# Samples' attention of a hybrid decoder layer: scores moved one step behind the key transposes, three PSUM banks for them, and the first gate block taken out of the Strassen loop

## The reference, cut to what matters

```python
def nsa_sample(nq, kvc, kvs, kvw, ngate, pool_c, pool_s, win_buf, page_table):
    ...
    o_c, imp = compressed_branch(qg, kc, q_pos)
    idx, valid = select_blocks(imp, q_pos, n_sel)
    ...
    o_s = sel_attend(qg, kv_sel, idx, valid, q_pos)
    o_w, win_new = window_sample(qg, win_buf, kvw, q_pos)
    return nsa_combine(o_c, o_s, o_w, ngate), win_new

def merge_out(o_hg, o_nsa, mgate, w_out):
    g = jax.nn.sigmoid(mgate.astype(jnp.float32)).reshape(B, T, N_BRANCH, D_MODEL)
    u = g[:, :, 0] * o_hg + g[:, :, 1] * o_nsa
    return u.astype(o_hg.dtype) @ w_out
```

## Time and profile before

| | |
|---|---|
| three runs, us | 1932.56, 1938.71, 1940.87 (median 1938.71) |
| the profiled execution: time / span of the trace, us | 1931.92 / 1930.1 |
| PE busy in the span | 1753.9 us (91%), 9667 matmuls |
| DVE, ACT, POOL busy | 49%, 27%, 33% |
| mean granted TensorE clock | 0.942 |
| samples' attention, first key transposes to first gate product | 855.1 to 1227.1 us |
| the eight gate blocks | 1227.1 to 1337.3 us |
| lines L2047, L2092, L2070 (PE busy) | 88.1, 83.3, 86.2 us |

### The profile page before, as it was taken

The page is one execution under the profiler, slowest core; times in us unless marked ns, Lnnn a source line. Parts: engine busy times, 40 slices in busy tenths (PEclk is TensorE's granted clock), DMA queues, the critical chain, the costliest instruction groups (busy, mean ns, idle before and its releaser), DMA issues.

```text
span 1930.1 us, 25763 instructions
## 1 busy us (share of the span) xinstructions
PE 1753.9 (91%) x9667; PEld 1229.7 (64%) x9667; DVE 953.7 (49%) x1702; ACT 522.8 (27%) x1114; POOL 634.5 (33%) x634
## 2 busy tenths in 40 slices
PE   7999999989979799976788887998989999999996
PEld 6777777777857555653555555776467777763332
DVE  6767776672000367753454445233267777760003
ACT  3122222221010245533444445211222222220101
POOL 2344443431000322235565552141045556530000
PEclk9999999998979579988999999999989999999998
DMA  8677666664430100014776677432043232311111
GB/s 262 217 241 241 230 204 227 229 207 163 109 118 4 45 1 1 2 45 148 220 227 208 211 227 235 128 110 87 28 109 88 66 88 66 88 66 54 66 41 49
DMA packets 201014, 248.81 MB, mean 129 GB/s; under 512 B 32201, under 2 KB 173850, under 8 KB 192538
## 3 DMA queue, kind: packets, MB, share of 16 engines
q1 hardware_dynamic: 176684, 134.16, 23.8%
q0 software_dynamic: 21248, 109.46, 16.5%
q10 hardware_dynamic: 2960, 3.54, 0.5%
HBM read 236.09 MB, written 19.29 MB: 132 GB/s over the span
## 4 chain that ended last, share of the span: by engine, by line
PE 74%; DVE 11%; DMA 5%; issue 4%; ACT 3%; another core or an unknown queue 2%; ACTq 1%; SPq 0%; POOL 0%; DVEq 0%; POOLq 0%
PE ps L2118 21%; PE ps L2244 8%; PE ps L1735 7%; DVE mem L1247 4%; PE ps L2070 4%; PE ps L1746 4%; DMA mem<-in_cache_cmp_kv,pidx 4%; PE ps L2092 3%; PE ps L2183 3%; PE ps L2047 3%; PE ps L1767 3%; PE ps L1975 2%; PE ps L1996 2%; PE ps L1962 2%
## 5 line engine op out<-in xcount | busy, mean ns | idle before, releaser
L2118 PE MATMUL ps<-mem 128*128 128x288 f32 x1352 | 338.2, 408 | 0.8 <-DVE mem L1185 0.8
L2118 PEld LDWEIGHTS ps<-mem 128*128 128x128 f32 x1352 | 256.2, 191 | 70.7 <-DVE mem L1185 1.0
L734 POOL DMA_INDIRECT mem<-in_cache_sel_kv,sidx x192 | 186.1, 969 | 322.0 <-PE ps L1928 174.3
L1735 PE MATMUL ps<-mem 128*128 128x288 f32 x1024 | 269.7, 426 | 14.7 <-DVE mem L1273 13.6
L1735 PEld LDWEIGHTS ps<-mem 128*128 128x128 f32 x1024 | 203.6, 200 | 73.7 <-issue 14.6
L1247 DVE TENSOR_TENSOR mem<-mem 128x2048 f32<-128x2048 f32 x56 | 159.6, 2850 | 43.3 <-DMA mem<-in_cache_cmp_kv,pidx 42.7
L697 POOL DMA_INDIRECT mem<-in_cache_cmp_kv,pidx x56 | 90.4, 1615 | 239.5 <-DVE mem L1247 210.6
L2244 PE MATMUL ps<-mem 128*128 128x512 f32 x352 | 163.7, 608 | 0.0
L2092 PE MATMUL ps<-mem 128*64 128x512 f32 x288 | 83.3, 654 | 61.0 <-ACT mem L1032 35.9
L1519 DVE TENSOR_TENSOR mem<-ps,mem 128x512 f32<-128x512 f32 x64 | 44.3, 692 | 153.4 <-PE ps L2092 92.2
L2244 PEld LDWEIGHTS ps<-mem 128*128 128x128 f32 x352 | 63.9, 191 | 80.7 <-issue 80.6
(11 more groups left out here) (363 smaller groups left out, 2687.2 us busy)
## 6 DMA issues: line engine op xcount, KB each, us to landing
mem<-in_cache_sel_kv SPq DMA_DIRECT2D x320, 128.0 KB
mem<-in_w_up SPq DMA_DIRECT2D x44, 512.0 KB, 5.1
mem<-in_w_in SPq DMA_DIRECT2D x32, 512.0 KB, 7.5
mem<-in_w_in SPq DMA_DIRECT2D x14, 1024.0 KB, 5.2
mem<-in_w_down SPq DMA_DIRECT2D x10, 1024.0 KB, 5.0
mem<-in_state_win_kv SPq DMA_DIRECT2D x16, 512.0 KB
out<-in_state_win_kv POOLq DMA_DIRECT2D x8, 1008.0 KB, 15.8
mem<-in_x_prompt SPq DMA_DIRECT2D x8, 512.0 KB, 5.4
```

What stands on the lines that cost most here:

```text
L734: pool.indirect_dma_start(kring[kq % NKR][:, j, :], None, pool_rows, bass.IndirectOffsetOnAxis(sidx[:, i:i + 1], 0)).then_inc(pg_g[kq % NK ...
L1735: mm = t.matmul(ps[:, 2 * (u % 2) + a, 0:NHF], lhs(k), hT[:, k, a * NHF:(a + 1) * NHF], start=(k == 0), stop=(k == KD - 1))
L2118: mm = t.matmul(ps[:, bank, 0:NHF], lhs[:, k, :], rhs[:, k, :], start=(first and k == 0), stop=(k == KD // 2 - 1), skip_group_check=True)
```

## The change

It renames and re-times, and computes the same.

- PE: the scores of step `s - 1` are issued in step `s`, after the values (`scores(n)`, called as the last piece before the compressed branch). The transposed keys go in two halves into three banks in turn (0, 1, 5; `KB`), each with its own semaphore step; probabilities have bank 4 alone.
- ACT: two copies of 512 columns instead of one of 1024, into three pairs of buffers; before the next transposes of probabilities PE waits for the copy of the last ones.
- `LAG` is 17 and `VAHEAD` 4. The exponentials move to `c` 1 to 4, DVE's scaling to 5 to 7. `e_c1`, `e_c3` move to `c` 1, 2; `e_c2` to 1, `e_c5` to 4, `e_c4`, `e_c6`, `e_c8`, `e_c10` to 2, 4, 6, 8. `e_out` stays tied to `LAG`.
- SP: the three blocks of gate weights come at `s` = 77, 79 and 81 instead of together at 80.
- The first gate block is done as 32 plain matmuls in two halves (`gate0`) in steps 84 and 86, with its sigmoids in ACT's steps 86 and 88; the loop of seven products has seven blocks left.

The diff, cut to its core (left out are re-numbered counts of `mp`, `mg_v`, `mg_a` in the gate loop, and the semaphores' names):

```diff
@@ -76,9 +76,9 @@
-LAG = NC + 6
+LAG = NC + 7
 K_POOL = (0, 1, 2)
-KAHEAD, VAHEAD = 4, 3
+KAHEAD, VAHEAD = 4, 4
...
@@ -217,7 +217,9 @@
-        kTs = [view(2 * PGC * P).rearrange("p (g n) -> p g n", g=2) for _ in range(2)]
+        kTs = [[view(PGC * P) for _ in range(2)] for _ in range(2)]
+        kTs.append([avm[:, :, :, :].rearrange("p i r c -> p (i r c)"), scanm[:, 0:PGC * P]])
+        KB = (0, 1, 5)
...
@@ -226,7 +228,7 @@
-        psm, psg, pscT = view(P), view(P), [view(P) for _ in range(2)]
+        psm, psg, pscT = view(P), view(P), [view(P) for _ in range(2)] + [hmask[:, :]]
...
@@ -478,7 +482,7 @@
-                return mp, 7 * (b - B_MG) + 7
+                return (mp, 7 * (b - B_MG)) if b > B_MG else (m0p, 2)
...
@@ -602,7 +606,7 @@
-                        wait(sp, ek_ok, kq - NKR + 1)
+                        wait(sp, ek_ok, 2 * (kq - NKR + 1))
...
@@ -610,10 +614,10 @@
-                if s == NC * SB:
-                    sp.wait_ge(ek_ok, SB * (NPC + 1))
-                    for b in range(B_MG, B_MG + NKR // 2):
-                        weights(b)
+                for n in range(NKR // 2):
+                    if s == NC * SB - 3 + 2 * n:
+                        sp.wait_ge(ek_ok, 2 * (SB * (NPC + 1) - NKR + 2 * n + 2))
+                        weights(B_MG + n)
...
@@ -752,12 +756,12 @@
-                        wait(pool, ek_ok, kq - NKR + 1)
+                        wait(pool, ek_ok, 2 * (kq - NKR + 1))
                         e_gather(kq)
             pool.wait_ge(es_ok, NC * SB)
-            for q in range(KD):
-                b = B_MG + q
+            for q in range(KD - 1):
+                b = B_MG + 1 + q
...
@@ -1000,9 +1004,9 @@
-                if b >= 2:
-                    act.wait_ge(epv_ok, NC * (b - 2) + 1)
-                a.activation(pscT[b % 2], cbank[:, 384:512], ACT.Copy).then_inc(c10_ok, 1)
+                if b >= 3:
+                    act.wait_ge(epv_ok, NC * (b - 3) + 1)
+                a.activation(pscT[b % 3], cbank[:, 384:512], ACT.Copy).then_inc(c10_ok, 1)
...
@@ -1025,40 +1029,45 @@
                 if b < SB and c <= NPC:
                     kq = b * (NPC + 1) + c
-                    act.wait_ge(ek_ok, kq + 1)
-                    if kq >= 2:
-                        bb, cc = divmod(kq - 2, NPC + 1)
+                    if kq >= 3:
+                        bb, cc = divmod(kq - 3, NPC + 1)
                         act.wait_ge(es_ok, NC * bb + cc + 1)
-                    a.activation(kTs[kq % 2], ps[:, 0:2, :], ACT.Copy).then_inc(ekT_ok, 1)
+                    for gp in range(2):
+                        act.wait_ge(ek_ok, 2 * kq + gp + 1)
+                        a.activation(kTs[kq % 3][gp], ps[:, KB[(2 * kq + gp) % 3], :], ACT.Copy).then_inc(ekT_ok, 1)
                 m = s - LAG
                 if m >= 0:
                     bb, cc = divmod(m, NC)
                     act.wait_ge(et_ok, m + 1)
                     wait(act, epv_ok, m - 1)
-                    src = ps[:, 4 + m % 2, :].rearrange("p (j q) -> p j q", q=P)
+                    src = ps[:, 4, :].rearrange("p (j q) -> p j q", q=P)
                     if cc < NC - 1:
                         ins = a.activation(pTs[m % 2], src, ACT.Copy)
                     else:
                         ins = a.activation(pTs[m % 2][0:S, 0:2, :], src[0:S, 0:2, :], ACT.Copy)
                     ins.then_inc(epT_ok, 1)
+                for x in range(2):
+                    if s == NC * SB + 6 + 2 * x:
+                        act.wait_ge(m0p, x + 1)
+                        a.activation(halves(mgb[x]), ps[:, 2 * x:2 * x + 2, 0:NHF], ACT.Sigmoid).then_inc(mge0_ok, 1)
                 if b + 1 < SB:
-                    if c == 3:
+                    if c == 1:
                         e_c2(b + 1)
-                    if c == 5:
+                    if c == 4:
                         e_c5(b + 1)
                     if c == 7:
                         e_c7(b + 1)
-                if c < 4 and 0 < b <= SB:
-                    e_exp(b - 1, [c] if c < 3 else [3, 4])
-            for q in range(KD):
-                m0, m1 = mgb[2 * (q % 2):2 * (q % 2) + 2]
+                if 1 <= c < 5 and 0 < b <= SB:
+                    e_exp(b - 1, [c - 1] if c < 4 else [3, 4])
+            for q in range(KD - 1):
+                m0, m1 = mgb[2 * ((q + 1) % 2):2 * ((q + 1) % 2) + 2]
                 act.wait_ge(mp, 7 * q + 1)
                 wait(act, mg_v, 5 * (q - 1) + 2)
                 a.activation(p1b, ps[:, 0, 0:NHF], ACT.Copy).then_inc(mg_a, 1)
                 act.wait_ge(mp, 7 * q + 4)
-                wait(act, u_hT, 2 * (q - 1))
+                wait(act, u_hT, 2 * q)
...
@@ -1498,15 +1507,15 @@
-                if s == NC * SB + 7:
+                if s == NC * SB + 8:
...
@@ -1540,16 +1549,16 @@
-                if 4 <= c < 7 and 0 < b <= SB:
-                    e_scale(b - 1, ([0, 1], [2, 3], [4])[c - 4])
+                if 5 <= c < 8 and 0 < b <= SB:
+                    e_scale(b - 1, ([0, 1], [2, 3], [4])[c - 5])
                 if b + 1 < SB:
+                    if c == 2:
+                        e_c4(b + 1)
                     if c == 4:
-                        e_c4(b + 1)
-                    if c == 5:
                         e_c6(b + 1)
-                    if c == 7:
+                    if c == 6:
                         e_c8(b + 1)
-                    if c == 9:
+                    if c == 8:
...
@@ -1558,11 +1567,14 @@
-                n, m = 2 * q + 1 - x, mgb[2 * (q % 2) + x]
+                m = mgb[2 * (q % 2) + x]
                 j = (2 * q + x) % KD
-                dve.wait_ge(mge_ok, n + 1)
-                if x == 0:
-                    dve.wait_ge(mg_a, 2 * q + 2)
+                if q == 0:
+                    dve.wait_ge(mge0_ok, x + 1)
+                else:
+                    dve.wait_ge(mge_ok, 2 * q - x)
+                    if x == 0:
+                        dve.wait_ge(mg_a, 2 * q)
...
@@ -2048,8 +2059,36 @@
+            def scores(n):
+                b, c = divmod(n, NC)
+                kq = b * (NPC + 1) + c
+                wait(pe, esc_ok, n - 1)
+                for gp in range(2):
+                    out = ps[64 * gp:64 * gp + 64, 2 + n % 2, :]
+                    if c <= NPC:
+                        pe.wait_ge(ekT_ok, 2 * kq + gp + 1)
+                        mm = t.matmul(out, qbd[:, b, gp, :], kTs[kq % 3][gp], start=True, stop=True)
+                    else:
+                        for br in range(2):
+                            mm = t.matmul(out[:, br * S:(br + 1) * S], qbd[:, b, gp, :], kT[:, br, gp, T:N], start=True, stop=True)
+                mm.then_inc(es_ok, 1)
             pe.wait_ge(on_ok, PT * NH // 2)
             pe.wait_ge(qbd_ok, 1)
+            def gate0(x):
+                w = wslot[B_MG % NSLOT].rearrange("p (k c) -> p k c", c=WB)
+                if x == 0:
+                    weights(B_MG)
+                    pe.wait_ge(ekT_ok, 2 * SB * (NPC + 1))
+                    pe.wait_ge(esc_ok, NC * SB)
+                for a in range(2):
+                    for k in range(KD):
+                        mm = t.matmul(ps[:, 2 * x + a, 0:NHF], w[:, k, x * P:(x + 1) * P], hT[:, k, a * NHF:(a + 1) * NHF],
+                                      start=(k == 0), stop=(k == KD - 1))
+                mm.then_inc(m0p, 1)
...
@@ -2064,40 +2103,34 @@
-                    wait(pe, ekT_ok, kq)
                     for gp in range(2):
+                        wait(pe, ekT_ok, 2 * kq + gp - 2)
+                        bank = KB[(2 * kq + gp) % 3]
                         for j in range(PGC):
-                            mm = t.transpose(ps[:, gp, j * P:(j + 1) * P], kring[kq % NKR][:, j, gp * P:(gp + 1) * P], ident[:, :])
-                    mm.then_inc(ek_ok, 1)
+                            mm = t.transpose(ps[:, bank, j * P:(j + 1) * P], kring[kq % NKR][:, j, gp * P:(gp + 1) * P], ident[:, :])
+                        mm.then_inc(ek_ok, 1)
                 if m >= 0:
                     pe.wait_ge(epn_ok, NP * bb + min(cc // 2, NP - 1) + 1)
-                    wait(pe, epT_ok, m - 1)
+                    wait(pe, epT_ok, m)
                     if cc < NC - 1:
                         o = cc * 512 if cc < NPC else SELW
                         for j in range(PGC):
-                            mm = t.transpose(ps[:, 4 + m % 2, j * P:(j + 1) * P], sc[bb % 2][:, o + j * P:o + (j + 1) * P], ident[:, :])
+                            mm = t.transpose(ps[:, 4, j * P:(j + 1) * P], sc[bb % 2][:, o + j * P:o + (j + 1) * P], ident[:, :])
                     else:
                         for j, o in enumerate((NPG * P, SELW + WIN)):
-                            mm = t.transpose(ps[0:S, 4 + m % 2, j * P:(j + 1) * P], sc[bb % 2][:, o:o + S], ident[:, :])
+                            mm = t.transpose(ps[0:S, 4, j * P:(j + 1) * P], sc[bb % 2][:, o:o + S], ident[:, :])
                     mm.then_inc(et_ok, 1)
                 if m >= 1:
```

(30 more changed lines are left out.)

31 lines of the change are left out of this document (16 added, 15 removed).

## The result

The changed kernel takes **1946.17 us** (median of 20 runs) beside 1939.75 for the kernel before (20 runs): ratio 1.0037, 95% interval 1.0022 to 1.0051. It is slower, by 6.4 us; the forecast was 38 us less. In two later sets the ratio was 1.0024 (1.0002 to 1.0046) and 1.0044 (1.0021 to 1.0068). Three executions far above the rest (8795 us in lag18_only, 2079 and 2289 us of the kernel before in the fourth set) are slow runs and left out of all that follows. The profiled span is 1942.9 us (clock 0.937) beside 1930.1 (0.942).

What follows compares the result with a forecast made beforehand. PE was taken as the bound, standing still 7 us a block. Terms of -28.7, -6.1, +3.2, +7.1 and -13.8 sum to -38.3 us against the median 1938.71: about 1901 us, range 1880 to 1932.

Steps and rivals of the forecast that it cites:

- Part 2: Five middle blocks: PE work 34.2 us plus two new waits and clock loss, 41.3 us a block; -6.1 us in all.
- Part 1: Steps 0 to 19: waits for ACT go, POOL's gathers set the pace; step 20 starts 28.7 us earlier.
- Parts 3, 4 and 5: Last block with scores +3.2 us, tail +7.1 us, seven Strassen gate blocks instead of eight -13.8 us.
- Part 4: Tail: window-page wait goes, plain first gate block comes in; 46.5 us for 39.4, so +7.1 us.
- The change does not do what it says: Rival: waits for ACT only move to the next key transposes, new waits come on top; 1956 us, chance 0.05.
- Supply: Rival: 9450 KB a block at 235 GB/s forbids blocks under 40.2 us; no chance of its own given.
- ACT becomes the bound: Rival: in steps with exponentials ACT makes five steps a block 0.8 us late each; 1925 us, chance 0.13.
- Slower by the clock: Rival: after the wait at c = 8 PE stays at the low level into the next block; 1967 us, chance 0.05.

Runs made afterwards that it cites:

- lag18_only: The changed kernel with LAG 18 alone, the output copy still a step late: 1939.02 us, ratio 1.0009 to the kernel before.
- the fourth set: Runs on one chip with prompt completions, of three kernels with register-indexed plain transfers; the kernel before took 1888.91 us there.
- out_lag18: The changed kernel with the output copy a step earlier and LAG 18, on a chip with prompt completions: 1856.47 us, ratio 0.9815.
- keys_fixed_pool: The changed kernel with output copy a step earlier, LAG 18, and POOL's gathers replaced by plain transfers from fixed rows: 1839.12 us (one run).
- regs_mended: The changed kernel with output copy a step earlier, LAG 18, and register-indexed plain transfers for POOL's gathers: 1849.66 us, ratio 0.9794.
- out_lag18_b: The changed kernel with output copy a step earlier and LAG 18, on a chip with late completions: 1922.73 us, ratio 0.9903.
- regs_before_b: The kernel before with register-indexed plain transfers for POOL's gathers, on a chip with late completions: 1875.13 us, ratio 0.9655.
- gate_only: The kernel before with only the gate part: plain first gate block, seven Strassen blocks, weight loads between last key steps: 1875.99 us, ratio 0.9927.
- regs_after: The changed kernel with register-indexed plain transfers in place of POOL's gathers: 1882.2 us, ratio 0.9954 to the kernel before.
- the regs pair: The kernel before and the changed kernel, both with register-indexed plain transfers for POOL's gathers: 1883.24 and 1882.2 us.
- scores_only: The changed kernel without its gate part, on a chip with prompt completions: 1900.36 us, ratio 1.0051 to the kernel before.
- out_early: The changed kernel with the output copy a step earlier, on a chip with prompt completions: 1865.47 us, ratio 0.9859.
- regs_mended_b: The changed kernel with output copy a step earlier, LAG 18 and register-indexed transfers, on a chip with late completions: 1843.75 us, ratio 0.9502.

## Why the prediction was wrong

**The step that failed** is the first of Part 2: "The work of PE in one is 34.7 us [...] I take 34.2", set against blocks of 42.5 us in the mean (212.6 for five), as if all the time in which PE stands still could be had by moving the scores. 34.2 is right as a floor where completions come at once (34.1 to 34.4 us in out_lag18, keys_fixed_pool and regs_mended). On a chip like that of the forecast it is not reached: with every misplaced step mended a block still takes 41.6 us in the mean (out_lag18_b). The 7.4 us between are late completions: the same kernel on the same chip with plain transfers in place of the gathers takes 34.1 (keys_fixed_pool). The rows for 34.2 could not show them: the last block and the earlier trace rows are from a time in which no gathers run, as the prediction says without drawing the conclusion, and the busy time of a block with gathers leaves a late signal out, since it shows as idle time.

The old order shows the same from the other side: it takes 35.6 us a block once completions come at once (regs_before_b, on a late chip), so of the forecast's 8.3 us (42.5 to 34.2) only 1.4 were to be had from the order of the steps. The wait for the copied keys was real, 26.9 us from 940 to 1120 us, but three quarters of it were late signals (7.7 us in gate_only), and such a wait does not go when the work is ordered anew: in out_lag18_b PE still waits some 22 us in the same stretch, for work of DVE and ACT at L2034, L2118, L2110 and L2058.

**Part 2, the waits.** Both were found, with place, releaser and cause. Their sizes: 1.5 us forecast for the transposes, 1.4 in regs_after (7.2 in five) and 2.9 at the longest in the changed kernel; 3.6 us for the output copy, 3.1 in regs_after (15.4 in five), and from 2.4 (shown) to 6.3 (the longest) in the changed kernel. For the clock 2 us were forecast; regs_after leaves 1.3 (39.9 less 34.1, 1.4 and 3.1), far from the full 3.6 us at each such wait that the prediction names beside its sum. Forecast for the block 41.3; regs_after 39.9; changed kernel 46.9 in the mean. So without late completions the block was sized to within 1.4 us, and on the late chip it is the floor of 34.2 in place of some 41 that is missing. In the regs pair Part 2 is the one part that comes out otherwise: 21.5 us more for the five blocks where 6.1 less were forecast.

**Part 1** (-28.7 us forecast) gave -8.8, for the same reason: the first 20 steps take 73.7 to 76.3 us in the changed kernel on late chips, and 54.4 to 55.5 with the same gathers on a prompt one (scores_only, out_early, out_lag18); the forecast said 56.4. The pace of POOL, 3.75 us for three gathers without waits, was right there. The sum was helped by luck: step 17 came 43 to 44 us after the first (47 forecast), and the three steps after it took 10.8 to 12.4 us (9.5 forecast). The gain there is 18.3 us (gate_only, in the old order, 72.7), not 28.7, since the old order is quicker on a prompt chip too (85.1 in the earlier trace rows). The regs pair, which has no gathers, gives -25.0 with the clock at 0.97 in place of 0.86. The 2 us for a set to land have no row: plain transfers on POOL's queue took a median of 3.7 us from issue to landing (regs_mended_b, 850 to 900 us).

**Parts 3, 4 and 5**: +3.2, +7.1 and -13.8 us forecast; +4.1, +4.8 and about -13.5 measured, +3.9, +6.8 and -13.6 in the regs pair. Right within 2.3 us. One slip is in Part 4: it counts 3 us of small waits for pages in words, but its sum, 46.5, does not hold them (with them it would be 49.5). In the changed kernel they hardly came: the tail took 44.14 us, of which PE stands still for only 0.8 (44.14 less 43.35).

**The rivals.** "The change does not do what it says" came nearest with its 1956 us, but by another mechanism: the waits for ACT went; ACT itself was told late. "Supply" forbade blocks under 40.2 us and seemed to hold on late chips (41 us in out_lag18_b); 278 GB/s in a block of 34.1 us on the same chip refute it. "ACT becomes the bound" did not come: 20.8 us busy of 34.1. "Slower by the clock" is part of it: in the middle block shown the clock is 0.89, where it was 1.00 in the earlier trace rows. No rival had signals that come late.

The Trainium skill ("GPSIMD Engine Reference", section 8, "Key points") calls GpSimd the only option for indirect DMAs. No run here tries another engine for them, but the indirection itself can be had otherwise: a row number read into a register and a plain transfer moved the same pages, with POOL busy for 1.71 us for three, where three gathers take 3.44 from first start to last end (1005.39 to 1008.83).

## What to carry to other kernels

When the order of one engine is moved by a step, move with it every step of the other engines that is tied to the same count, and place each by who waits for it: one copy left a step behind cost 5.2 us a block, and with the scaling it undid what the first blocks had gained (21.5 of 25.0 us in the regs pair). A floor for a block has to be read where everything that runs in it runs, the other queues' transfers too; a quieter block is no control. And when an engine starts 3 or 4 us after the work it waits for seems done, ask what holds the signal before ordering the work anew.
